# A row tile for each bias table, and the compressed keys' projection in two weight blocks

## The reference

```
# bias of a table by distance, for "a" (heads 0..7) and "b" (heads 8..15)
bias   = rel_bias[t5_bucket(dist)]
logits = q @ k / 8 + bias
# compressed keys and values of "a": 2 groups of 64 columns each
kc, vc = h @ w_in[:, 512:640], h @ w_in[:, 640:768]
blk    = z[:, :, win_idx] + cmp_pos[which]      # windows of 32 tokens, stride 16
hid    = gelu(blk.reshape(.., 32 * 64) @ cmp_w1[which])
out    = hid @ cmp_w2[which]
```

## Time and profile before

| | |
|---|---|
| median of 3 runs | 1597.78 us (1594.37 to 1599.24) |
| profiled execution | 1595.08 us |
| its span, first to last instruction | 1593.3 us |
| mean granted clock of PE | 0.981 |
| PE busy | 1492.8 us (94%) |
| DVE busy | 1002.5 us (63%) |
| ACT busy | 768.8 us (48%) |
| POOL busy | 67.7 us (4%) |

### The profile page before, as it was taken

How to read it: one execution, slowest core, us unless ns; L and a number is a source line. 1 busy time by engine, 2 the same in 40 slices (tenths; PEclk the granted TensorE clock), 3 DMA queues, 4 the chain that set the end, 5 groups by cost and what they waited for, 6 DMA issues and landing times.

```text
span 1593.3 us, 24198 instructions
## 1 busy us (share of the span) xinstructions
PE 1492.8 (94%) x9392; PEld 1212.9 (76%) x9392; DVE 1002.5 (63%) x2306; ACT 768.8 (48%) x1642; POOL 67.7 (4%) x76
## 2 busy tenths in 40 slices
PE   6999998999999999999988997888899999989999
PEld 4777756787778777888766776666688889789987
DVE  3647677464667458535575666766786657677753
ACT  4436576353556343241133535565666437455542
POOL 0000000010000000020000100001101020000000
PEclk9999999999999999999989998999999999999999
DMA  9131162222452232221461153423435552445553
GB/s 355 54 106 54 48 244 94 73 93 79 139 188 85 79 107 86 93 80 53 146 238 53 53 166 87 133 90 129 152 127 172 179 196 94 145 146 188 190 191 133
DMA packets 60130, 203.89 MB, mean 128 GB/s; under 512 B 7714, under 2 KB 10988, under 8 KB 59888
## 3 DMA queue, kind: packets, MB, share of 16 engines
q1 hardware_dynamic: 53856, 193.89, 35.6%
q10 hardware_dynamic: 5984, 7.40, 2.1%
q0 software_dynamic: 176, 1.06, 0.2%
HBM read 200.47 MB, written 1.84 MB: 127 GB/s over the span
## 4 chain that ended last, share of the span: by engine, by line
PE 73%; DVE 14%; ACT 5%; DMA 4%; issue 3%; POOL 1%; ACTq 0%; SPq 0%; POOLq 0%; DVEq 0%
PE ps L2207 67%; PE ps L2210 5%; DVE w_l L2870 3%; DVE st L2966 1%; DMA w_raw<-in_l_out 1%; DVE x L2878 1%; ACT l_P L2518 1%; ACT w_h L2515 1%; DMA w_l_ada<-in_l_ada 1%; DVE l_h_lat L2878 1%; DMA m_biasb<-m_vec 1%; DVE l_xn L2874 1%; DVE l_P L2874 1%; DMA w_raw<-in_m_aq 1%; POOL mstat L3544 0%
## 5 line engine op out<-in xcount | busy, mean ns | idle before, releaser
L2870 DVE TENSOR_TENSOR w_l<-w_raw,w_h 128x1024 fp32r<-128x1024 f32 (+3 forms) x265 | 317.1, 1205 | 75.3 <-ACT w_h L2515 74.7
L2515 ACT ACTIVATE w_h<-w_raw 128x1024 fp32r<-128x1024 f32 (+3 forms) x265 | 273.3, 1042 | 110.8 <-DMA w_raw<-in_l_out 26.5
L2207 PE MATMUL ps<-w_h,l_hTh 128*128 128x512 f32 (+1 forms) x384 | 157.4, 410 | 0.5 <-DVE w_l L2870 0.5
L2207 PE MATMUL ps<-w_h,l_hTl 128*128 128x512 f32 (+1 forms) x384 | 153.2, 399 | 0.0
L2207 PE MATMUL ps<-w_l,l_hTh 128*128 128x512 f32 (+1 forms) x384 | 153.1, 399 | 0.0
L2518 ACT ACTIVATE l_P<-ps,st 128x512 f32<-128x512 f32 (+1 forms) x128 | 77.6, 608 | 91.8 <-DVE st L2878 64.7
L2207 PE MATMUL ps<-f_hTh,w_h 128*128 128x256 f32 x352 | 99.1, 281 | 0.0
L2207 PE MATMUL ps<-l_hTh,w_h 128*128 128x512 f32 (+1 forms) x264 | 98.5, 373 | 0.5 <-issue 0.5
L2966 DVE TENSOR_REDUCE st<-ps 128x1 f32<-128x512 f32 (+2 forms) x112 | 72.7, 649 | 41.7 <-PE ps L2207 41.0
L2207 PE MATMUL ps<-f_hTl,w_h 128*128 128x256 f32 x352 | 98.9, 281 | 0.0
L2207 PE MATMUL ps<-f_hTh,w_l 128*128 128x256 f32 x352 | 98.8, 281 | 0.0
(11 more groups left out here) (443 smaller groups left out, 3507.8 us busy)
## 6 DMA issues: line engine op xcount, KB each, us to landing
w_raw<-in_l_ada SPq DMA_DIRECT2D x81, 512.0 KB, 4.3
w_raw<-in_l_z SPq DMA_DIRECT2D x32, 512.0 KB, 3.6
w_raw<-in_l_out SPq DMA_DIRECT2D x32, 512.0 KB, 3.8
w_raw<-in_m_merge SPq DMA_DIRECT2D x24, 512.0 KB, 3.2
w_raw<-in_f_gate SPq DMA_DIRECT2D x22, 512.0 KB, 4.3
w_raw<-in_f_up SPq DMA_DIRECT2D x22, 512.0 KB, 4.3
w_raw<-in_f_down SPq DMA_DIRECT2D x22, 512.0 KB, 4.4
w_raw<-in_l_q SPq DMA_DIRECT2D x16, 512.0 KB, 3.7
```

The source lines that it names most:

```text
L2207: return p.e.matmul(out, lhsT, rhs, start=start, stop=stop)
L2515: return p.e.activation(out, a, func, scale=scale)
L2870: return p.e.tensor_tensor(out, a, b, op)
```

## The change

The second kind, "a", gets a row tile of its own (`veca`), on the bytes of the selection `ohb`. `mix_vec` no longer waits for the transfer of table "b" before it copies the row for "a". The weight array `m_cmp` becomes two blocks of 128 different columns in place of four blocks of 64 columns twice. `proj_cmp` evacuates two groups from each bank: for both, ACT copies the same 64 partitions of the bank once to the lower half of `kc2` and once, shifted by one token, to the upper half; both position updates then follow in two successive pending steps. The chain woven into the attention of "b" has 28 pieces instead of 32, and the weave's rate is set to 28 by 13.

```diff
--- before.py
+++ after.py
@@ -98,7 +98,7 @@
         add(f"m_{name}", "w_in_2", [_r(a, a + 512)], 2, D, pick=lay0)
     add("m_bkv", "w_in_2", [np.concatenate([_r(1816, 2072), _r(1280, 1304), _r(3608, 3616)])], 2, D, pick=lay0)
     add("m_akv", "w_in_2", [np.concatenate([_r(768, 896), _r(1024, 1152), _r(896, 1024), _r(1152, 1280)])], 2, D, pick=lay0)
-    add("m_cmp", "w_in_2", [np.tile(_r(a, a + 64), 2) for a in (512, 576, 640, 704)], 8, D, pick=lay0)
+    add("m_cmp", "w_in_2", _split(_r(512, 768), 128), 8, D, pick=lay0)
     add("m_merge", "w_in_2", _split(_r(3616, 6688), 128), 8, D, pick=lay0)
     for x in range(2):
         add(f"cmp_w1{x}", "cmp_w1_2", [_r(0, 256)], 4, 2048, pick=lambda a, x=x: a[0, x])
@@ -865,7 +865,7 @@
         m.flush()
         f = p.fence()
         m.bias("a", f)
-        weave(m.attend("b", f, 4), chain(m.proj_akv(f), m.proj_q("a", f, [LAT]), m.proj_cmp(f), m.branch("c", f)), 32, 13)
+        weave(m.attend("b", f, 4), chain(m.proj_akv(f), m.proj_q("a", f, [LAT]), m.proj_cmp(f), m.branch("c", f)), 28, 13)
         m.flush()
         weave(m.compress(f, (2, 3)), chain(m.gates("b"), m.branch("b", f)), 24, 20)
         m.flush()
@@ -1851,7 +1851,7 @@
         self.gain = new("gain", [128, 3, 64], 1024)
         self.gb, self.tab = new("gains", [128, 6, 64], 1792), new("tab", [33, 16], 3328)
         self.oh = {"a": new("oha", [33, 384], 3392), "b": new("ohb", [33, 384], 4928)}
-        self.vec = new("vec", [8, 384], 6464)
+        self.vec = {"b": new("vecb", [8, 384], 6464), "a": new("veca", [8, 384], 4928)}
         self.scr = {k: n.scratch(f"m_bias{k}", (32, 8, 384)) for k in "ba"}
         self.fscr = n.scratch("m_c", (8, 256))
         self.hm, self.sel4, self.row31 = sm[:, 16:24], sm[:, 24:56], sm[:, 56:57]
@@ -1976,12 +1976,12 @@
         p = self.p
         p.mix_pos0(self, fence)
 
-        def evac(g, b, tok):
-            a = ("comp", "in", g)
-            p.mix_pos_in(self, a, g, b, tok, fence)
+        def evac(w, b, tok):
+            a = ("comp", "in", w)
+            p.mix_pos_in(self, a, w, b, tok, fence)
             p.give(b, a)
-            self.later.append([None, lambda: p.mix_pos(self, g, a)])
-        yield from self.projected(p.dense_ch("m_cmp", 0, 4, 8, 128, self.hT, 0, 256, evac))
+            self.later.append([None, lambda: p.mix_pos(self, 2 * w, a), lambda: p.mix_pos(self, 2 * w + 1, a)])
+        yield from self.projected(p.dense_ch("m_cmp", 0, 2, 8, 128, self.hT, 0, 256, evac))
 
     def forget(self, fence):
         p = self.p
@@ -2745,11 +2745,13 @@
         p.wait_ge(tok, fence)
         p.copy(m.gz[:, t, :], ps[:, 256:288]).then_inc(*p.mark("mix", "gz", t))
 
-    def mix_pos_in(p, m, key, g, b, tok, fence):
-        ps = p.n.bank(b, 256)
+    def mix_pos_in(p, m, key, w, b, tok, fence):
         p.wait_ge(tok, fence)
-        p.copy(m.kc2[0:64, g, :], ps[0:64, :])
-        p.copy(m.kc2[64:128, g, 0:255], ps[64:128, 1:256]).then_inc(*p.mark(*key))
+        for gg in range(2):
+            ps = p.n.bank(b, 256)[64 * gg:64 * gg + 64]
+            p.copy(m.kc2[0:64, 2 * w + gg, :], ps)
+            a = p.copy(m.kc2[64:128, 2 * w + gg, 0:255], ps[:, 1:256])
+        a.then_inc(*p.mark(*key))
 
     def fg_exp(p, m, fence):
         e = m.f[1]
@@ -2843,7 +2845,7 @@
 
     def mix_diag(p, m, k):
         p.wait_ge(("mix", "vec", k))
-        p.e.dma_start(m.scr[k].rearrange("p h m -> h p m"), m.vec[:].unsqueeze(1).to_broadcast([8, 32, 384])).then_inc(*p.landed("d_diag", k))
+        p.e.dma_start(m.scr[k].rearrange("p h m -> h p m"), m.vec[k][:].unsqueeze(1).to_broadcast([8, 32, 384])).then_inc(*p.landed("d_diag", k))
 
     def mix_bias(p, m, k, fence):
         p.wait_ge(("d_diag", k), fence)
@@ -3275,8 +3277,8 @@
         p.ts(m.small[:, 8:16], m.small[:, 0:8], -1.0, ALU.mult).then_inc(*p.mark("mix", "sink"))
 
     def mix_vec(p, m, b, k):
-        p.wait_ge(("mix", "vec_mm", k), ("d_diag", "b") if k == "a" else None)
-        p.copy(m.vec[:], p.n.ps[0:8, b, 0:384]).then_inc(*p.mark("mix", "vec", k))
+        p.wait_ge(("mix", "vec_mm", k))
+        p.copy(m.vec[k][:], p.n.ps[0:8, b, 0:384]).then_inc(*p.mark("mix", "vec", k))
 
     def norm_total(p, m, key, x, nh, a, qs_free, tmp, fence):
         st, sq = m.small[:, 64 + 16 * x:64 + 16 * x + 16], m.sq[x][:, 0:nh * 64]
```

## The result

| | before | changed |
|---|---|---|
| median | 1596.80 us (7 runs, 1588.86 to 1599.49) | 1581.70 us (7 runs, 1579.51 to 1590.42) |
| profiled execution, span | 1593.3 us | 1579.9 us |
| mean granted clock of it | 0.981 | 0.984 |

The ratio is 0.9928 with a 95% interval of 0.9909 to 0.9947, so the change takes off 11.5 us (8.5 to 14.5). The medians lie 15.1 us apart, the two spans 13.4. The same changed kernel, run once more beside others (`after_again`), gave 0.9891 (0.9865 to 0.9916).

A forecast was written before the change was run, and what follows sets the result against it. TensorE (PE), busy 94% of the span, was taken as the bound, with a stall at 953 to 965 us. 9.3 + 4.6 = 13.9 us off 1597.78 gave 1583.9, rounded 1584; range 1578 to 1590.5.

The forecast's parts named there:

- the wait at the tile: Layer 3, DVE's copy of row "a" waiting for table "b"'s transfer: removing it saves 9.3 us (6.8 to 11.3).
- the projection: Attention "b" stage, two blocks of compressed-key weights for four: net 4.6 us saved (2.4 to 5.6).
- Part 1, the meeting of DVE and PE: Fifth unit's maximum: PE 9.44 us earlier, DVE 8.6, DVE just the later; maximum at 963.45, 9.3 us earlier.
- my high end: Removed tile wait: 8.6 + 2.65 = 11.3 us, if the clock is paid for beside the wait.
- Part 1, the transfers: Table "a" beside table "b" and two weight loads: 5.4 us landing, 2.3 us slack, costed at nothing.
- Part 2, PE's work: Attention "b" stage: 48 matmuls of 256 columns fewer at 0.1165 us each, 5.6 us.
- Part 2, the evacuation: Four ACT copies per bank, 0.38 to 1.05 us each: PE waits 0 to 1.2 us, taken as 0.5.
- Part 2, the denser weave: Attention "b" stage, 2.15 pieces of cover per step for 2.46: a quarter of 2.1 us waits added, 0.5 us.
- The attention is the bound: Rival in the "b" stage: the projection change gives nothing, 1588.5 us; chance 0.13.
- The clock gives more: Rival: the second clock fall, in 985 to 986, goes too, 18.9 us saved, 1579; chance 0.08.
- The transfers take the place of the wait: Rival: two tables and weights collide, 3.8 us; the tile change keeps some 2.9, 1590.3; chance 0.05.
- slower: Rival: less cover in 1200 to 1262, PE's waits bring the clock to 1.2 GHz, up to 1638; chance 0.03.

The follow-up runs named there:

- vec_only: Kernel before with only the separate row tile for "a", compressed projection as before; 1587.67 us, ratio 0.9939.
- cmp_only: Changed kernel with the shared row tile and its wait put back, so the two-block projection alone; 1592.16 us, ratio 0.9976.
- before_fill: Kernel before plus 28 unread matmuls of 512 columns filling PE's idle time ahead of layer 3's third unit's scores; 1596.63 us, ratio 1.000.
- late_w14: Changed kernel with position updates put off by five pieces and the weave at 28 by 14; 1580.69 us, ratio 0.9900.
- pos_late: Changed kernel with the position updates on DVE put off by five more pieces of the weave; 1577.02 us, ratio 0.9895.
- evac_split: Changed kernel with two of each bank's four evacuation copies, those from the upper 64 partitions, moved from ACT to DVE; 1582.58 us, ratio 0.9906.
- early_only: Kernel before, shared tile and wait kept, each row's table transfer issued right after its copy, one step earlier; 1585.37 us, ratio 0.9934.
- weave32: Changed kernel with the weave's rate back at 32 by 13, so the 28 pieces run out earlier; 1581.72 us, ratio 0.9914.
- after_early: Changed kernel with table "b"'s transfer issued some 12 us earlier, right behind its row's copy; 1582.20 us, ratio 0.9918.
- late_early: Changed kernel with position updates put off by five pieces and table "b"'s transfer issued early; 1580.79 us, ratio 0.9910.
- late_early_w14: Changed kernel with position updates put off by five pieces, early table "b" transfer and weave at 28 by 14; 1579.40 us, ratio 0.9901.

## Why the prediction came out

**Forecast.** 1584 us was forecast, as 13.9 us off; measured were 1581.7, and 11.5 us off by the ratio. The two sizes that went into the 13.9 stand against what each part alone and the profiles showed:

| term | forecast | measured |
|---|---|---|
| the wait at the tile | 9.3 | 9.3 (stretch 68.2 to 58.9); 9.7 by the ratio of `vec_only` |
| the projection | 4.6 | 3.2 (stage 61.7 to 58.5; 3.0 by the means of four profiles each); 3.8 by the ratio of `cmp_only` |
| sum | 13.9 | 12.5 |

The 12.5 lie within the 8.5 to 14.5 of the ratio, and the 13.4 of the two spans are 12.5 and 0.9 that sit elsewhere. That the first term agrees to a tenth is luck: the same subtraction gives 8.1 to 9.6 us, according to where the clock fell in the executions compared.

**Part 1, the meeting of DVE and PE.** Right in place and, as near as the clock lets one say, in size. The copy came at 953.17, the first maximum at 953.94, PE did not idle, and the fifth maximum came at 963.04 (forecast: 963.45). That DVE is the later of the two was shown by `before_fill`. With PE at full clock through the stall, only 1.0 us of the 10.11 went. Adding the clock's 2.65 us to DVE's wait, my high end, would have been wrong.

**Part 1, the transfers.** The place was right and the size was not. I priced the two weight loads at 5.4 us each, with 2.3 us of slack. The row of issues of the changed kernel, for the two of 960 to 969.8, says 7.5 us, for 3.5 in the earlier trace rows:

```profile
w_raw<-in_l_z SPq DMA_DIRECT2D x2, 512.0 KB, 7.5
```

The first took 8.13. So the slack of 2.3 us was used up: ACT came free at 972.31 and started at 972.43, and PE waited 1.90 us there, for 1.67 in the earlier trace rows:

```profile
974.03 0.75 PE L2210 MATMUL ps<-identr,l_qs 128*128 128x128 f32 x4 [1.90 <-ACT l_PTs L2515]
```

The cost is 0.2 us, near the nothing that I put down. The seven profiles that have the second tile and the late transfer show the edge: where the first load took 7.6 to 7.7 us (four of them), PE waited 1.66 to 1.68 us, as before; with 8.1 and 8.2 it was 1.90 and 1.94, and with 8.37 in `late_w14` 2.13:

```profile
963.85 8.37 DMA w_raw<-in_l_z
```
```profile
973.84 0.53 PE L2210 MATMUL ps<-identr,l_qs 128*128 128x128 f32 x4 [2.13 <-ACT l_PTs L2515]
```

So from 8.13 to 8.37 PE's wait grew one for one with the landing time, and the right price in place of nothing was 0 to 0.5 us of PE's wait. The Trainium skill ("DMA: Bandwidth & Descriptors", section "Queues, rings and completion order") has each DMA engine take turns between the queues that have work; the landing times of 8.13 us for the first of the two loads and 7.5 for their median, issued with table "a" still in flight, for 3.5 without, agree with it.

**Part 2, PE's work.** 48 matmuls fewer, 5.6 us forecast; the busy time of the stage fell by 5.3.

**Part 2, the evacuation.** Copies from one half of the partitions to the other were bounded by 0.38 and 1.05 us each. The row by tile of the changed kernel has them at the low end, the same as in the earlier trace rows:

```profile
L2515 ACT ACTIVATE m_kc<-ps x8: 360/378/383, 1228.3 to 1234.3; 64x256 f32<-64x256 f32 x4, 64x255 f32<-64x255 f32 x4
```

Four in a row took 1.53 and 1.55 us, and PE waited 0.6 for them, for a forecast of 0.5.

**Part 2, the denser weave.** This is the term that was mis-sized. I added a quarter of the waits of the earlier trace rows, 0.5 us. The waits grew by 4.3 - 2.1 = 2.2 us in all; less the 0.6 of the evacuation that is 1.6 us, three times what I put down. A wait doesn't scale with cover. Pieces moved against the attention's steps, and two new waits came up: 1.8 us for `m_ak` and 1.3 us for `m_tm`. The second has its cause in the change itself, the two position steps in succession, which I had passed over with "keep their count". `pos_late` shows it by taking it away. The 1.8 us for `m_ak` is there in every kernel with 28 pieces over 13 steps (the changed one, `cmp_only`, `pos_late`, `evac_split`), and isn't at the rate of 32 by 13 (the kernel before, `vec_only`, `early_only`, `weave32`). With 14 steps PE waits the same 1.8 us for another transpose's input, `m_P`; what in the order makes it I did not take apart.

**Rivals.** *The attention is the bound* (part 2 gives nothing) fell, but a part of it was true: PE handed back 2.1 of its 5.3 us as idle time. *The clock gives more*: the second fall stayed in the changed kernel's profile, at 975, and such a fall is worth 1.7 us, not the 2 that I estimated. *The transfers take the place of the wait*: they used up the slack, and cost 0.2 us beyond it. *No change* and *slower* fell; the stage ran at a granted clock of 1.00 with waits of up to 1.8 us, though one of 2.09 in `evac_split` had a fall behind it, and one of 2.35 in `weave32` had none.

## What to carry to other kernels

A wait that one engine does for the sake of a shared tile costs what stands behind it in that engine's order; look for it as idle time ahead of a cheap copy, and remove it by a second tile or by issuing the transfer earlier; both together gave no more here. When work is taken off the engine that sets the pace, count on a part coming back as waits for the others, and look at batches of short instructions (here four updates and a weight rest) in front of the one that gives a bank back. A transfer that moves earlier moves into other traffic: compare the slack of each load that it meets with a landing time of more than twice the undisturbed one (7.6 to 8.4 us here beside table "a" as in the changed kernel, and 8.5 to 10.0 where table "b" was issued early, for 3.5).

## What the runs showed of the hardware

**A fall of the clock loses 1.7 us of full clock, and its places change from execution to execution.** In slices of 1 us over the whole span, each fall of the granted clock from 1.00 to 0.50 and back loses a sum of 1.7 us of full clock (some come as two at once, 3.4, and the stall of the kernel before as three, 5.1; one is cut off by the end of the span). The same PE wait for `l_PTs`, of 1.7 to 2.1 us, has a fall in it or behind it in seven of the fourteen profiles and none in the other seven. First PE's list and the slice of 1 us behind it in the second profile of the changed kernel (the four transposes take 0.74 us):

```profile
967.99 0.74 PE L2210 MATMUL ps<-identr,l_qs 128*128 128x128 f32 x4 [1.66 <-ACT l_PTs L2515]
```
```profile
969.00:970.00 1.00, 1.00 (x4) 0.73 (x3) 1.00 (x2) 1.00 (x5) 0.00 (x0) 0.50 0.00 0
```

Then both in `weave32` (0.53 us), where the code up to there is the same:

```profile
974.21 0.53 PE L2210 MATMUL ps<-identr,l_qs 128*128 128x128 f32 x4 [1.67 <-ACT l_PTs L2515]
```
```profile
975.00:976.00 1.00, 1.00 (x6) 0.63 (x4) 1.00 (x2) 1.00 (x5) 0.00 (x0) 1.00 0.00 0
```

Summed over the profile, 31.0 us were lost so before, 26.0 in the changed kernel's first profile and 22.7 in its second. The two profiles of the changed kernel have spans of 1579.9 and 1574.5, and 3.3 of these 5.4 us are such falls.

**The span times its mean granted clock is the steadier number.** Over the seven runs of the changed kernel the span has a standard deviation of 3.6 us and the product one of 1.1; over 25 runs of the kernel before it is 2.8 and 1.9. The clock of a run is recorded to 0.001, which is 1.6 us of the product. The product's means:

| | mean of span x clock, us | runs |
|---|---|---|
| before (four sets) | 1562.0, 1561.3, 1561.1, 1561.8 | 25, 9, 11, 11 |
| changed (two sets) | 1553.6, 1554.3 | 7, 6 |
| `before_fill` | 1565.9 | 12 |
| `cmp_only` | 1558.4 | 12 |
| `early_only` | 1558.2 | 6 |
| `vec_only` | 1556.9 | 8 |
| `weave32` | 1556.6 | 4 |
| `after_early` | 1555.9 | 6 |
| `evac_split` | 1555.3 | 4 |
| `late_early` | 1555.1 | 6 |
| `late_early_w14` | 1553.7 | 4 |
| `late_w14` | 1553.5 | 6 |
| `pos_late` | 1553.2 | 4 |

The two sets of the changed kernel, 0.37% apart as ratios, agree within 0.7 us. Their mean clocks were 0.9824 and 0.9853, and 0.0029 of 1580 us is 4.6. `weave32` is 2.6 us above their mean of 1554.0, beside a stage longer by 2.2; `pos_late` is 0.8 below it, beside one shorter by 1.0. Each of the four kernels with the early transfer lies above its partner without it, by 1.3 (`early_only` over `vec_only`), 1.9, 1.9 and 0.2 us, which agrees with the rounding's waits of 1.76 to 3.18 us for the load that the transfer delays; none of these distances is clear of the scatter by itself. The number misleads where the clock is low while PE idles: in the kernel before, the stall lost 5.1 us of clock by the slices but only 1.0 of time, so the product makes it look some 4 us too fast, as `before_fill` shows (1565.9 for 1562.0, at the same time). Why the clock falls behind a wait in one execution and not in the next, no run here settles.
